# Mixer attention steps: state-space products spread over eight steps and alternated with the gates' dense products, results stored in two halves

## The reference, cut to what matters

```python
proj = h @ w_in                        # u, q, k, v, f, g_a, g_b
y_ssm = s5_ssm(u, ...)                 # 32 groups of 16 channels, 64 states each
z_val, z_gate = split(gelu(y_ssm) @ glu_w)
y_a = z_val * sigmoid(z_gate)
attn = forgetting_attention(q, k, v, f + forget_b)    # 8 heads, causal
y_b = attn @ attn_w_out
merged = sigmoid(g_a) * y_a + sigmoid(g_b) * y_b
return merged @ w_out
```

## Time and profile before

| | |
|---|---|
| time, median of 3 runs | 3523.5 us (3518.73 to 3524.08) |
| time of the profiled execution | 3520.14 us |
| its span in the profile | 3518.4 us |
| PE busy | 3338.8 us, 95% of the span |
| DVE, POOL, ACT busy | 2012.8, 1340.8, 1175.5 us |
| mean granted TensorE clock | 0.959 of full |

### The profile page before, as it was taken

How to read it: one execution, slowest core, us unless ns; L and a number is a source line. 1 busy time by engine, 2 the same in 40 slices (tenths; PEclk the granted TensorE clock), 3 DMA queues, 4 the chain that set the end, 5 groups by cost and what they waited for, 6 DMA issues and landing times. The chain is left out here.

```text
span 3518.4 us, 44582 instructions
## 1 busy us (share of the span) xinstructions
PE 3338.8 (95%) x16330; PEld 2609.5 (74%) x16330; DVE 2012.8 (57%) x2706; ACT 1175.5 (33%) x1792; POOL 1340.8 (38%) x565
## 2 busy tenths in 40 slices
PE   8999999999996999899998999879998999999997
PEld 6657787657775888788776888768887877778886
DVE  3876685876685444996374442244459954654412
ACT  3354323355323223333334222232233324332232
POOL 3302343302333445443152445434454431534453
PEclk9999999999997999999899999989999998999999
DMA  4524472523453332586142332133234951423321
GB/s 130 169 76 125 118 239 70 170 78 121 132 189 89 95 92 83 95 112 109 49 123 61 107 95 81 57 107 95 86 91 82 124 99 46 135 72 95 92 86 61
DMA packets 587985, 363.85 MB, mean 103 GB/s; under 512 B 58146, under 2 KB 537772, under 8 KB 587564
## 3 DMA queue, kind: packets, MB, share of 16 engines
q1 hardware_dynamic: 583988, 355.21, 39.1%
q10 hardware_dynamic: 3832, 6.42, 0.5%
HBM read 346.63 MB, written 12.58 MB: 102 GB/s over the span
## 5 line engine op out<-in xcount | busy, mean ns | idle before, releaser
L152 POOL TENSOR_TENSOR w_lo<-w_raw,w_hi 128x1024 fp32r<-128x1024 f32 (+2 forms) x552 | 1332.8, 2420 | 2130.7 <-ACT w_hi L144 2130.7
L158 PE MATMUL bank<-xh,w_lo 128*128 128x512 f32 x2432 | 982.1, 404 | 45.3 <-DVE xl L2353 25.2
L160 PE MATMUL bank<-xh,w_hi 128*128 128x512 f32 x2432 | 966.5, 397 | 0.0
L159 PE MATMUL bank<-xl,w_hi 128*128 128x512 f32 x2432 | 964.2, 396 | 0.0
L144 ACT ACTIVATE w_hi<-w_raw 128x1024 fp32r<-128x1024 f32 (+2 forms) x552 | 566.1, 1029 | 797.4 <-PE bank L160 730.4
L158 PEld LDWEIGHTS bank<-xh,w_lo 128*128 128x128 f32 x2432 | 465.2, 191 | 167.0 <-issue 42.4
L159 PEld LDWEIGHTS bank<-xl,w_hi 128*128 128x128 f32 x2432 | 465.7, 191 | 104.5 <-issue 4.3
L160 PEld LDWEIGHTS bank<-xh,w_hi 128*128 128x128 f32 x2432 | 464.9, 191 | 103.2
L158 PE MATMUL bank<-HH,w_lo 128*128 128x512 f32 x704 | 278.6, 396 | 0.0
L160 PE MATMUL bank<-HH,w_hi 128*128 128x512 f32 x704 | 278.5, 396 | 0.0
L159 PE MATMUL bank<-HL,w_hi 128*128 128x512 f32 x704 | 278.4, 395 | 0.0
(11 more groups left out here) (506 smaller groups left out, 4536.6 us busy)
## 6 DMA issues: line engine op xcount, KB each, us to landing
w_raw<-in_ffn_w_in_dram SPq DMA_DIRECT2D x176, 512.0 KB, 3.8
m_raw_l<-in_mod_w_dram SPq DMA_DIRECT2D x128, 512.0 KB, 5.0
w_raw<-in_w_in_dram SPq DMA_DIRECT2D x80, 512.0 KB, 4.0
w_raw<-in_mix_w_in_dram SPq DMA_DIRECT2D x64, 512.0 KB, 9.2
w_raw<-in_ffn_w_out_dram SPq DMA_DIRECT2D x64, 384.0 KB, 3.5
w_raw<-in_ffn_w_out_dram SPq DMA_DIRECT2D x64, 320.0 KB, 3.1
m_half_l<-in_mod_w_dram SPq DMA_DIRECT2D x32, 256.0 KB, 2.7
w_raw<-in_w_out_dram SPq DMA_DIRECT2D x16, 512.0 KB, 4.9
```

Source lines behind the costliest of these rows:

```text
L152: nc.gpsimd.tensor_tensor(ring.lo[s][:, 0:width], ring.raw[s][:, 0:width], ring.hi[s][:, 0:width].bitcast(F32), ALU.subtract).then_inc(rin ...
L158: nc.tensor.matmul(out, wl, xh, start=start, stop=False)
L159: nc.tensor.matmul(out, wh, xl, start=False, stop=False)
L160: return nc.tensor.matmul(out, wh, xh, start=False, stop=stop)
```

## The change

The four `y_product` are taken apart. Steps 0 to 7 each call `y_and_gate(step)`, which does half of one (four groups, 12 matmuls) together with the step's whole share of the gates, matmul by matmul: a dense product, `Mt`, a dense product, `Cr`, a dense product, `Ci`. Groups of a step beyond its number of gate slices stand alone behind them: one in steps 0, 1, 3 and 4, two in steps 2 and 5, none in 6 and 7. So 24 of a layer's 32 groups are alternated and 8 stand alone. ACT's `take_chunk` moves to steps 1, 3, 5 and 7, and comes after the step's dense products, before ACT's evacuation of a gate. The waits for `Mt` and the states move to step 0.

`Yc` is stored in two halves of 8 DMAs each, the first after the second quarter (step 3), the other after the fourth (step 7); the read back is two DMAs, both issued behind the second store. The waits of the GELU follow. The turned probabilities use bank 4 alone until step 7, and steps 6 and 7 keep their scores between the two transposes.

```diff
-    YS = 2
+    YN = 8
-    for j in range(2 * YS + 8):
+    for j in range(2 * YN):
         hold(("t", j), 4)
...
+        def y_half(i):
+            wait_read(sp, ("y", 2 * i + 1))
+            g = slice(i * GP, (i + 1) * GP)
+            for t in range(CH):
+                sp.dma_start(yv[:, CH - 1 - t, g, :], Yc[t * SG:(t + 1) * SG, g, :]).then_inc(s[f"y_out{i}"], 16)
+        def y_back(i):
+            sp.wait_ge(s[f"y_out{i}"], 16 * 8)
+            sp.dma_start(ych[:, 2 * i:2 * i + 2, :, :].rearrange("p t s c -> p t (s c)"),
+                         y_dram.rearrange("(t p) c -> p t c", p=P)[:, 2 * i:2 * i + 2, :]).then_inc(s[f"y_in{i}"], 16)
         for i in range(3):
             merge_block(i)
-        wait_read(sp, ("y", 3))
...
-        for i in range(3, 10):
+        y_half(0)
+        merge_block(3)
+        y_half(1)
+        y_back(0)
+        y_back(1)
+        for i in range(4, 10):
             merge_block(i)
...
+        def y_and_gate(step):
+            f, ks = parts[step]
+            i, at = step // 2, step % 2 * 4
+            if step == 0:
                 pe.wait_ge(s["m_in"], 16 * 32)
                 pe.wait_ge(s["states"], 4)
+            out = free(pe, ("y", i)) if at == 0 else held(("y", i))
+            gated = free(pe, ("g", f)) if 0 in ks else held(("g", f))
+            wh, wl = weights(B_G + f, f % 4)
+            for n in range(4):
+                g = 16 * (i // 2) + 2 * (at + n) + i % 2
                 r = slice(g % 2 * SP_, g % 2 * SP_ + SP_)
+                o = out[:, (at + n) * NC:(at + n + 1) * NC]
+                dense = n < len(ks)
+                if dense:
+                    k = ks[n]
+                    cc = slice(k * P, k * P + P)
+                    nc.tensor.matmul(gated, wl[:, cc], xh[:, k, :], start=k == 0, stop=False)
                 nc.tensor.matmul(o, Mt[:, g, :], U[:, g, :], start=True, stop=False)
+                if dense:
+                    nc.tensor.matmul(gated, wh[:, cc], xl[:, k, :], start=False, stop=False)
                 nc.tensor.matmul(o, Cr[r, g // 2, 0:8, :]..., Xr[r, g // 2, :], start=False, stop=False)
+                if dense:
+                    last = nc.tensor.matmul(gated, wh[:, cc], xh[:, k, :], start=False, stop=k == KT - 1)
...
                 last = nc.tensor.matmul(o, Ci[r, g // 2, 0:8, :]..., Zi[r, g // 2, :], start=False, stop=True)
+            if at:
+                last.then_inc(s["chunk_out"], 1)
...
             turn_probs(2 * g)
-            if g < YS + 4:
+            if g < YN:
                 scores(g + 2)
             turn_probs(2 * g + 1)
-            if YS + 4 <= g < NS - 2:
+            if YN <= g < NS - 2:
                 scores(g + 2)
-            if YS <= g < YS + 4:
-                y_product(g - YS)
-            gate_parts(g)
+            if g < YN:
+                y_and_gate(g)
+            else:
+                gate_parts(g)
             attend(g)
...
-                act.wait_ge(s["y_in"], 16)
+                act.wait_ge(s[f"y_in{t // 2}"], 16)
...
-                if YS <= g < YS + 4:
-                    take_chunk(g - YS)
+                if g < YN and g % 2:
+                    take_chunk(g // 2)
```

More of the change, by code:

```diff
@@ L1479, in second_block @@
              "b_powers", "b_turned", "c_powers", "k_taps", "m_cleared", "m_in", "u_out", "u_in", "injected",
-             "states", "chunk_out", "gate_out0", "gate_out1", "gate_in0", "gate_in1", "y_out", "y_in", "y_sum", "gelu_square", "gelu_arg", "gelu_tanh",
+             "states", "chunk_out", "gate_out0", "gate_out1", "gate_in0", "gate_in1", "y_out0", "y_out1", "y_in0", "y_in1", "y_sum", "gelu_square", "gelu_arg", "gelu_tanh",
              "skip_added", "z_split", "f_split", "f_logits", "f_biased", "f_exp", "f_log", "cum_ready", "scores", "maxima",
@@ L1539, in second_block @@
         hold(("s", j), j % 4)
-        if j >= 2 * YS + 8:
+        if j >= 2 * YN:
             hold(("t", j), 4 + j % 2)
@@ L1706, in _ @@
             gate(f)
+        yv = y_dram.rearrange("(g m) (t c) -> m t g c", m=SG, t=CH)
+        def y_half(i):
[7 more added lines that the diff above has]
+                         y_dram.rearrange("(t p) c -> p t c", p=P)[:, 2 * i:2 * i + 2, :]).then_inc(s[f"y_in{i}"], 16)
         for i in range(3):
             merge_block(i)
-        wait_read(sp, ("y", 3))
[L1710 to L1714, removed]
-        for i in range(3, 10):
+        y_half(0)
[4 more added lines that the diff above has]
+        for i in range(4, 10):
             merge_block(i)
@@ L1967, in scores @@
                 nc.tensor.matmul(out[side][:, q * P:n], ident_r[:, :], mask_r[:, :], start=False, stop=True).then_inc(s["scores"], 1)
-        def y_product(i):
-            if i == 0:
+        def y_and_gate(step):
+            f, ks = parts[step]
+            i, at = step // 2, step % 2 * 4
+            if step == 0:
                 pe.wait_ge(s["m_in"], 16 * 32)
                 pe.wait_ge(s["states"], 4)
-            out = free(pe, ("y", i))
-            for g8 in range(8):
-                g = 16 * (i // 2) + 2 * g8 + i % 2
-                r = slice(g % 2 * SP_, g % 2 * SP_ + SP_)
-                o = out[:, g8 * NC:(g8 + 1) * NC]
+            out = free(pe, ("y", i)) if at == 0 else held(("y", i))
[3 more added lines that the diff above has]
+                g = 16 * (i // 2) + 2 * (at + n) + i % 2
+                r = slice(g % 2 * SP_, g % 2 * SP_ + SP_)
+                o = out[:, (at + n) * NC:(at + n + 1) * NC]
[4 more added lines that the diff above has]
+                    nc.tensor.matmul(gated, wl[:, cc], xh[:, k, :], start=k == 0, stop=False)
                 nc.tensor.matmul(o, Mt[:, g, :], U[:, g, :], start=True, stop=False)
+                if dense:
+                    nc.tensor.matmul(gated, wh[:, cc], xl[:, k, :], start=False, stop=False)
                 nc.tensor.matmul(o, Cr[r, g // 2, 0:8, :].rearrange("p j m -> p (j m)"), Xr[r, g // 2, :], start=False, stop=False)
+                if dense:
+                    last = nc.tensor.matmul(gated, wh[:, cc], xh[:, k, :], start=False, stop=k == KT - 1)
+                    if k == KT - 1:
+                        last.then_inc(ring.used, 1)
                 last = nc.tensor.matmul(o, Ci[r, g // 2, 0:8, :].rearrange("p j m -> p (j m)"), Zi[r, g // 2, :], start=False, stop=True)
-            last.then_inc(s["chunk_out"], 1)
+            if at:
+                last.then_inc(s["chunk_out"], 1)
         def turn_probs(j):
```

## The result

| | before | after |
|---|---|---|
| median of 4 runs | 3521.11 us | 3550.75 us |
| lowest to highest | 3518.65 to 3524.08 | 3535.16 to 3567.61 |
| profiled execution, span | 3520.14, 3518.4 us | 3535.16, 3533.3 us |

The changed kernel is slower in these runs. The ratio of the times is 1.0087 with a 95% interval of 1.0059 to 1.0116. The mean granted clock of each of the four executions goes with its time: 0.960, 0.956, 0.955 and 0.951 for 3535, 3547, 3554 and 3568 us. The profiled one is the fastest of them. Ratios here leave out an execution more than 1.5% above its kernel's fastest, which matters for one number only (`e9_again`).

The account below looks back on a forecast made before the run. PE was taken to set the pace in steps 0 to 7. Per mixer −16.2 + 7.4 + 0.9 = −7.9 us; two mixers −15.8, one slow spell +4: −11.8 us, from 3523.5 to 3512 us, range 3500 to 3533.

Parts of the forecast that it names:

- The clock afterwards: Steps 0 to 7: clock stays full through most, with one half-clock spell of about 9.4 us in two mixers, costing 4 us.
- The sign that the prediction itself named: Steps 0 to 7: the prediction is wrong if the clock row still shows half clock inside alternated groups.
- Rival (a): Steps 0 to 7: the clock falls in the alternated mix as well, kernel 3544 us; chance 0.15, partial form 0.07.
- The point where (a) turns the sign: Steps 0 to 7: half-clock time at which the gain becomes a loss, 18 us per mixer.
- the prediction's own length of a mixer at full clock: Steps 0 to 7 of one mixer: 85.49 − 16.2 + 8.3 us, with alternating and the ACT wait included.
- What the slow clock cost before: Steps 0 to 7 before the change: half clock for 37.6 us per mixer, losing 16.2 us, to be won back.
- The cost of alternating: Alternated groups at full clock: 2.03 us each against 1.64, from four row changes instead of two; adds 7.4 us per mixer.
- The sum, not the overlap: Dense product between two row changes: the two extra costs add, giving 0.43 us, rather than overlap, giving 0.34.
- The rule of the Trainium skill: TensorE's next weights load behind the running matmul; kept as rival (b), row changes free, 3480 us, chance 0.05.
- The wait on ACT: Step 6, before the second transposes: PE waits for bank 4 behind ACT's work, 0.9 us per mixer, bounds 0 and 1.7.
- Stores and read back: SP issues the second half's stores in 4.8 us; read back lands 8.5 us into step 8, 1.7 us before needed.

Follow-up runs that it names:

- e9_again: The changed kernel itself run once more, for a second trace and its spread; median 3526.6 us over ten runs, ratio 1.0022 to the kernel before.
- e5_no_lone: The changed kernel with a step's dense matmuls shared out over all 12 state-space matmuls, so no group stands alone; 3566.6 us, ratio 1.0136 to the kernel before.
- e1_triples: The changed kernel with each alternated group as three dense products, then its three state-space matmuls, two row changes instead of four; 3487.0 us, ratio 0.9913 to before.
- e6_even_triples: e1_triples with a step's dense products shared out evenly before its four groups, so no group stands alone; 3483.8 us, ratio 0.9916 to the kernel before.
- e2_spread: The changed kernel without alternation: in each of eight steps four groups in a run, then the step's gate slices; 3505.6 us, ratio 0.9966 to before.
- e8_four_changes: e1_triples with `Cr` and `Mt` exchanged, so a group has four row changes but dense products stay in threes; 3552.2 us, ratio 1.0091 to before.
- e4_rows128: The changed kernel with `Cr` and `Ci` products replaced by further `Mt` products, no row changes, state part not computed; 3468.0 us, ratio 0.9867 to before.
- e7_rows_grouped: e6_even_triples with `Mt` among the dense products and a step's eight 64-row products together behind them; 3476.1 us, ratio 0.9875 to before; its repeat 3476.0 us.

## Why the prediction was wrong, step by step

- **The step that failed is "The clock afterwards".** It took one spell of 9.4 us for the two mixers together, from the length of the runs of state-space products without a dense one between, and full clock in the alternated groups. The trace had 73.6 us at half clock, as much as before (75), so the gain of 32.4 us for both mixers did not come and the cost of alternating was left. The steps missed the forecast by 26.9 us (+15.1 against −11.8): 64.2 us more at half clock, at 0.43 us lost per microsecond, are 27.6. The sign that the prediction itself named, half clock inside alternated groups, is there (1671.40 to 1674.91). Its reasoning tied the fall to bare runs of small products; e5_no_lone has no state-space run longer than two products and fell for 92 us on end. What the runs put in its place: with dense products among the groups, the three orders with 112 changes of rows a mixer had 73.6 to 142 us at half clock in both mixers together, those with 64 had 6.8 and 0 (e1_triples, e6_even_triples), those with 16 or none had none. The count of changes is not all: e2_spread and the kernel before have 64 as well, in runs of four and eight groups without a dense product, and had 47.8 and 75 us.
- **Rival (a) was the one that came**, at a chance of 0.15. Its remark that a fallen clock finds no stretch to rise in before step 8 was right in part. Before, a spell lasted 6.8 to 10.2 us, and the first mixer's four all ended within 1.7 us of the end of the 6 or 9 dense products behind a `y_product`. In the alternated mix spells of 20.5, 41.0, 58.0 and 92.2 us occur, beside others of 3.4 and 6.8, and most do end inside the eight steps. The error was in the number more than in the length: six spells instead of one, of 12.5 us on average instead of 9.4.
- **The point where (a) turns the sign** was right: 18 us at half clock per mixer. The second mixer had 20.5 and came out at 85.9 against 85.5. The price of 0.43 us lost per microsecond at half clock held too: 77.6 + 0.43 × 53.1 = 100.4 against 100.18 measured, and 77.6 + 0.43 × 20.5 = 86.4 against 85.88. The 77.6 is the prediction's own length of a mixer at full clock.
- **What the slow clock cost before**, 16.2 us per mixer: about right. e6_even_triples keeps the clock, has the old two changes a group, and needs 68.5 us against 85.5. That is 17.0 less, or 17.7 without the 0.67 us of waiting on ACT that before has not.
- **The cost of alternating**, 7.4 us per mixer: a little low. A group takes 2.04 us (2.03 predicted). By the steps, the second mixer less its slow clock is 85.88 − 0.43 × 20.5 = 77.1 us (an estimate), against 67.9 in e1_triples without its wait: 9.2. The two small errors, here and in the 16.2, cancel. The sum, not the overlap, is right for the dense product with a change on both sides (0.43). The swap in e8 shows the price once more from the other side, 0.33 for two changes.
- **The rule of the Trainium skill** (TensorE: Matmul & The Clock Gate, Part 2) that the next weights load behind the running matmul holds between products of 128 rows, as far as e4_rows128 shows: its 1.35 to 1.37 us a group leave no time for a load beyond what the nine matmuls cost among their like. Across a change of rows time is lost: standing between two changes costs the small pair 0.14 us (0.36 against 0.22) and the dense product 0.20 (0.43 against 0.23). The Trainium skill (TensorEngine Tiling (Array Packing), Key Properties) says that a change of the tiling mode drains TensorE. These prices are in line with it; no run shows a drain as such.
- **The wait on ACT** in step 6, 0.9 us: right in kind. It is in e1_triples' timeline, 0.67 us of idle before the second transposes, released by ACT's copy, behind exactly the four ACT instructions named:

```profile
1685.46 0.44 PE L1981 MATMUL bank<-mask_r,ident_r 128*128 128x128 f32 x2
1686.57 0.52 PE L2014 MATMUL bank<-tables_sb,th 128*128 128x128 f32 x3 [0.67 <-ACT PT L2264]
```

```profile
1684.01 0.60 ACT L2231 ACTIVATE Yc<-bank 128x512 f32<-128x512 f32 x1 [3.12 <-PE bank L2005]
1684.51 0.59 ACT L2210 ACTIVATE stg<-bank 128x512 f32<-128x512 f32 x1
1684.99 1.06 ACT L144 ACTIVATE w_hi<-w_raw 128x1024 fp32r<-128x1024 f32 x1
...
1685.93 0.49 ACT L2264 ACTIVATE PT<-bank 128x384 f32<-128x384 f32 x1
```

  In the changed kernel's first trace it is hidden, since PE was at half clock there and later than ACT. In its second trace the first mixer's step 6 begins at full clock, and there it stands:

```profile
1727.30 0.44 PE L1981 MATMUL bank<-mask_r,ident_r 128*128 128x128 f32 x2
1728.41 0.52 PE L2019 MATMUL bank<-tables_sb,th 128*128 128x128 f32 x3 [0.68 <-ACT PT L2269]
```

- **Stores and read back**: right. The timeline of SP, after:

```profile
1694.79 3.81 SPq L1714 DMA_DIRECT2D y_scratch<-Yc  x8
...
1745.84 4.66 SPq L1714 DMA_DIRECT2D y_scratch<-Yc  x8
1750.54 2.25 SPq L1719 DMA_DIRECT2D ych<-y_scratch  x2
```

  The second half was issued in 4.66 us (4.8 predicted). The read backs landed 3.8 to 5.6 us after their issue, the first one so 7.4 us into step 8 (8.5 predicted) and 3.4 us before its reader at 1757.9; in the second mixer it was 1.9 us before. ACT never waited for them.
- **The size.** The forecast was 3512 us in 3500 to 3533. The profiled execution's 3535 is explained by the clock in the steps, as above. The median of 3551 lies among slower executions; their mean clocks were lower, but where in the execution is not known. The second set's median of 3527 falls inside the range, by luck: its trace has 88.8 us at half clock in the steps, not 9.4.

## What to carry to other kernels

Where PE sets the pace, count the changes of rows between neighbouring matmuls before alternating two kinds. At full clock one cost 0.13 us here when whole steps are compared (e6_even_triples to e7_rows_grouped, 6.3 us for 48 changes) and up to 0.19 when groups are (2.04 against 1.66 us for two). Put matmuls of one row count together: e7_rows_grouped and its repeat are 42 and 47 us faster than before with the same products. Then ask what the order does to the clock, and price both ends: neither the number nor the length of the old spells holds for a new order. Times that spread wide are a hint and no proof of such a stretch: the changed kernel ran over 56 us in ten executions, but e1_triples, with one short spell in its trace, over 33 as well, and before over 20.

## What the runs showed of the hardware that was not expected

The clock stayed at half for 92.2 us on end while PE was busy for 116.48 of 116.88 us (e5_no_lone). The Trainium skill's advice to keep TensorE busy without gaps (TensorE: Matmul & The Clock Gate, its table on why this matters) is not enough here: the trace shows 0.4 us of idle in that mixer, and half the clock. One exchange of two neighbouring matmuls of 64 columns (e8_four_changes against e1_triples) moved the median by 65 us. Of the 59 us by which the steps of the two traces differ, 24 × 0.33 × 2 = 16 us are the changes' own cost at full clock, and 99.3 us more at half clock, at 0.43, are the other 43. And identical instructions in one execution had 53 us at half clock in one mixer and 20 in the other; what decides that was not tried and stays open, as does what exactly the clock follows.
